# Recurrent layer: the tokens of odd chunks lie from last to first, and two chunks share each level product

## What is computed

```
def step(s, inp):                       # one chunk of one head
    qc, kc, vc, gc = inp
    cum = jnp.cumsum(gc, axis=2)        # log decay since the chunk's start, per key channel
    o_inter = einsum('bhtk,bhkv->bhtv', qc * exp(cum), s)
    decay = exp(where(causal, cum[:, :, :, None] - cum[:, :, None], -inf))
    att = einsum('bhtk,bhsk,bhtsk->bhts', qc, kc, decay)
    o = o_inter + einsum('bhts,bhsv->bhtv', att, vc)
    last = cum[:, :, -1:, :]
    s_new = exp(last)[..., None] * s + einsum('bhsk,bhsv->bhkv', kc * exp(last - cum), vc)
    return s_new, o
```

## Time and profile before

| | |
|---|---|
| median of 3 runs | 1660.47 us (1659.8 to 1665.47) |
| profiled execution | 1659.53 us, span 1657.8 us |
| PE, weight loads | 1600.0 us (97%), 1203.3 us (73%) |
| DVE | 1069.9 us (65%) |
| ACT, POOL | 651.3 us (39%), 450.1 us (27%) |
| mean granted TensorE clock | 0.988 of full speed |

### The profile page before, as it was taken

One profiled execution on the slowest core, in us unless ns is written; L12 is line 12 of the kernel. 1 busy time (PEld: TensorE's weight loads), 2 busy tenths in 40 slices (PEclk: granted clock), 3 DMA queues, 4 the chain that ended last, 5 costly groups with the idle time before them and its releaser, 6 DMA issues.

```text
span 1657.8 us, 24332 instructions
## 1 busy us (share of the span) xinstructions
PE 1600.0 (97%) x9089; PEld 1203.3 (73%) x9089; DVE 1069.9 (65%) x1962; ACT 651.3 (39%) x1252; POOL 450.1 (27%) x336
## 2 busy tenths in 40 slices
PE   6999999999999999997899999999999999998997
PEld 4788888888888887444677777777777777774543
DVE  7578787968787776213537675868777676766321
ACT  4324243424333342212145555555555455555100
POOL 5021223222122200002124343524253434323200
PEclk9999999999999999998999999999999999999999
DMA  9581819273645643423032444445453645356231
GB/s 269 151 235 60 254 42 280 61 233 104 191 131 163 207 139 117 116 74 132 13 108 77 158 151 138 137 143 166 153 166 129 194 136 185 146 193 227 89 140 40
DMA packets 254086, 242.35 MB, mean 146 GB/s; under 512 B 23162, under 2 KB 219962, under 8 KB 253970
## 3 DMA queue, kind: packets, MB, share of 16 engines
q1 hardware_dynamic: 242834, 204.21, 40.1%
q0 software_dynamic: 11136, 36.59, 6.4%
HBM read 212.63 MB, written 95.24 MB: 186 GB/s over the span
## 4 chain that ended last, share of the span: by engine, by line
PE 85%; DVE 10%; ACT 2%; issue 2%; DMA 0%; SPq 0%; POOL 0%; DVEq 0%; ACTq 0%; POOLq 0%
PE psum L1923 42%; PE psum L1947 7%; PE psum L2418 6%; PE psum L2000 6%; PE psum L2239 4%; PE psum L2216 4%; PE psum L2223 4%; PE psum L2272 2%; PE psum L1911 2%; PE psum L2178 2%; PE psum L2040 1%; PE psum L2061 1%; PE psum L2012 1%; PE psum L2054 1%; DVE arena L1265 1%
## 5 line engine op out<-in xcount | busy, mean ns | idle before, releaser
L1923 PE MATMUL psum<-arena 128*128 128x252 f32 (+1 forms) x3472 | 828.1, 389 | 5.5 <-DVE arena L1275 3.7
L1923 PEld LDWEIGHTS psum<-arena 128*128 128x128 f32 x3472 | 649.6, 193 | 131.1 <-issue 30.4
L1275 DVE TENSOR_TENSOR arena<-arena,psum 128x252 f32<-128x252 f32 (+1 forms) x310 | 130.5, 421 | 227.8 <-PE psum L1923 218.9
L816 POOL TENSOR_TENSOR arena<-arena 128x1024 f32<-128x1024 f32 x64 | 155.4, 2429 | 224.6 <-DMA arena<-k_pages 204.7
L1095 ACT ACTIVATE arena<-psum,arena 128x256 f32<-128x256 f32 (+7 forms) x128 | 93.8, 739 | 130.8 <-DVE arena L1613 130.5
L892 ACT COPY arena<-psum 128x252 f32<-128x252 f32 (+1 forms) x124 | 46.0, 371 | 235.3 <-PE psum L1923 235.3
L679 POOL TENSOR_TENSOR arena<-arena 128x512 f32<-128x512 f32 x31 | 41.0, 1323 | 292.2 <-issue 145.5
L2418 PE MATMUL psum<-arena 128*128 128x512 f32 x256 | 114.3, 597 | 0.0
L1947 PE MATMUL psum<-arena 128*128 128x512 f32 x256 | 112.7, 594 | 0.1
L2000 PEld LDWEIGHTS psum<-arena 128*128 128x128 f32 x896 | 108.1, 192 | 4.4 <-issue 1.0
L2000 PE MATMUL psum<-arena 128*128 128x64 f32 x896 | 106.1, 271 | 0.0
(11 more groups left out here) (255 smaller groups left out, 2140.8 us busy)
## 6 DMA issues: line engine op xcount, KB each, us to landing
k_pages<-in_cache_k SPq DMA_DIRECT2D x64, 512.0 KB, 6.5
v_pages<-in_cache_v SPq DMA_DIRECT2D x64, 512.0 KB, 7.1
arena<-k_pages SPq DMA_DIRECT2D x64, 512.0 KB, 3.5
arena<-v_pages SPq DMA_DIRECT2D x64, 512.0 KB, 5.4
arena<-in_w_in_a SPq DMA_DIRECT2D x32, 512.0 KB, 7.1
arena<-in_x_prompt SPq DMA_DIRECT2D x16, 512.0 KB, 6.1
arena<-in_w_kv SPq DMA_DIRECT2D x16, 512.0 KB, 5.7
arena<-in_w_in_b SPq DMA_DIRECT2D x16, 512.0 KB, 7.2
```

Of the source, the lines that this page charges most:

```text
L816: pool.tensor_tensor(k_ring[:, m % 2], k_ring[:, m % 2], q_all[:, m % S:m % S + 1, :].broadcast_to([P, PAGES, P]), ALU.mult).then_inc(kq_m ...
L1275: dve.tensor_tensor(out, more, bank[n % 2][:, 0:size(u)], ALU.add).then_inc(of.by_dve, 1)
L1923: ins = pe.matmul(bank[n % 2][:, 0:size(u)], w[:, k, :], x[:, k, :], start=(k == 0 and r in (0, 1, 3, 4)), stop=(k == HK - 1), skip_group_ ...
```

## The change

Chunks are stored in another order: the even chunks (0, 2, 4, 6) fill the first 512 columns, the odd chunks (1, 3, 5, 7) the second 512, and within an odd chunk the tokens lie from last to first. In a block of 2w columns of an odd chunk the earlier tokens (keys) now lie in the upper half, where in an even chunk they lie in the lower half. So the keys' halves of an even and an odd chunk interleave to one full array of 128 weight columns, and the queries' halves of both make 128 moving columns. `level(w)` on PE forms 4 products of 128 x 128 in place of 8 of 128 x 64; of each result, the quarter of even keys by even queries and that of odd keys by odd queries is used, chosen by the mask.

What follows from it: `x_out` writes odd tiles mirrored; the scan is two scans, the second from the last column to the first; `split` and `factors` run over even and odd chunks as an outer pair and write dense arrays; `merge` is two predicated copies of 256 columns; the masks have 128 columns a level instead of 64, the keep mask half its length; the end sums of the chunks are read from other places; the state updates and outputs take their chunk by `block_of`; `o_all` writes the odd chunks mirrored back, in three instructions instead of one; and the output projection takes tile t from `rows_of(t)`.

```diff
...
 SPLIT = (0, 252, HN)
+MID = T // 2
+def block_of(c):
+    return c % 2 * (NC // 2) + c // 2
+def mirrored(ap):
+    return bass.AP(ap.tensor, ap.offset + C - 1, [*ap.ap[:-1], [-1, C]])
+def pairs_of(ap, w, even, odd, wide=True):
+    return bass.AP(ap.tensor, ap.offset + even, [ap.ap[0], [odd - even, 2], [2 * w, MID // (2 * w)], [1 if wide else 0, w]])
 def spans(u):
...
         spare_at = used[0]
-        level_mask = area(len(LEVELS) * UPPER)
-        chunk_keep = area(T // 2).bitcast(BF16)
+        level_mask = area(len(LEVELS) * P)
+        chunk_keep = area(T // 4).bitcast(BF16)
         gain_a = area(KT)
...
         k_dec = logf[:, 0:T]
+        chunk_sums = bass.AP(cum.tensor, cum.offset + C - 1, [cum.ap[0], [MID - C + 1, 2], [C, NC // 2]])
         diffs, facts = area(2 * T), area(2 * T)
...
         prompt_out = io["state_prompt"].rearrange("l b h k v -> (l b h) k v")
+        def rows_of(t):
+            return cols(block_of(t) if t < TT else t)
         def cols(t):
...
             for l, w in enumerate(LEVELS):
-                m = level_mask[:, l * UPPER:(l + 1) * UPPER].rearrange("p (b w) -> p b w", w=w)
+                m = level_mask[:, l * P:(l + 1) * P].rearrange("p (x b w) -> p x b w", x=2, w=w)
                 last = pool.affine_select(out=m, in_=m, compare_op=ALU.is_ge, fill=0.0, base=0,
-                                          pattern=[[-2 * w, UPPER // w], [0, w]], channel_multiplier=1)
+                                          pattern=[[-w, 2], [-2 * w, UPPER // w], [0, w]], channel_multiplier=1)
             last.then_inc(built.sem, 1)
...
             pool.affine_select(out=keep, in_=keep, compare_op=ALU.not_equal, fill=0.0, base=0,
-                               pattern=[[0, NC], [1, C]], channel_multiplier=0).then_inc(built.sem, 1)
+                               pattern=[[0, NC // 2], [1, C]], channel_multiplier=0).then_inc(built.sem, 1)
             pool.wait_ge(built.sem, built.at("masks1"))
             for l, w in enumerate(LEVELS):
-                m = level_mask[:, l * UPPER:(l + 1) * UPPER].rearrange("p (b w) -> p b w", w=w)
+                m = level_mask[:, l * P:(l + 1) * P].rearrange("p (x b w) -> p x b w", x=2, w=w)
                 last = pool.affine_select(out=m, in_=m, compare_op=ALU.is_ge, fill=0.0, base=w - 1,
-                                          pattern=[[2 * w, UPPER // w], [0, w]], channel_multiplier=-1)
+                                          pattern=[[w, 2], [2 * w, UPPER // w], [0, w]], channel_multiplier=-1)
             last.then_inc(built.sem, 1)
...
                 act.activation(f_smp, logf[:, T:N], ACT.Exp)
-                act.activation(dec, cum[:, C - 1::C], ACT.Exp).then_inc(acts.sem, 1)
+                act.activation(dec.rearrange("p (x i) -> p x i", x=2), chunk_sums, ACT.Exp).then_inc(acts.sem, 1)
                 level(32)
...
                     src = bank[2 + 2 * (t % 2) + j][:, :].rearrange("p (k n) -> p k n", n=P)[:, :, 0:rows]
-                    dve.tensor_tensor(x_t[:, 4 * j:4 * j + 4, cols(t)], src,
+                    dst = x_t[:, 4 * j:4 * j + 4, rows_of(t)]
+                    dve.tensor_tensor(mirrored(dst) if t < TT and t % 2 else dst, src,
                                       gain_a[:, 4 * j:4 * j + 4].unsqueeze(2).broadcast_to([P, 4, rows]),
...
                 dve.tensor_tensor(h_new[n // 2][:, half], res[n // 2][:, half], bank[n % 2], ALU.add).then_inc(part_taken, 1)
+            def by_chunk(ap):
+                return ap.rearrange("p (i s) -> p i s", s=C)
             def o_all(h):
...
                     dve.wait_ge(o_stored, 16 * (h - 1))
-                dve.tensor_tensor(o_t[:, AH - 2 + h % 2, :], o_rs, sg_h, ALU.mult).then_inc(o_done, 1)
+                out = o_t[:, AH - 2 + h % 2, :]
+                dve.tensor_tensor(out[:, 0:MID], o_rs[:, 0:MID], sg_h[:, 0:MID], ALU.mult)
+                dve.tensor_tensor(mirrored(by_chunk(out[:, MID:T])), by_chunk(o_rs[:, MID:T]), by_chunk(sg_h[:, MID:T]), ALU.mult)
+                dve.tensor_tensor(out[:, T:N], o_rs[:, T:N], sg_h[:, T:N], ALU.mult).then_inc(o_done, 1)
             def head(h):
...
                 def split(w):
-                    c = cum.rearrange("p (b w) -> p b w", w=2 * w)
-                    d = diff[LEVELS.index(w) % 2].rearrange("p (b w) -> p b w", w=2 * w)
-                    mid = c[:, :, w - 1:w].broadcast_to([P, T // (2 * w), w])
-                    dve.tensor_tensor(d[:, :, w:2 * w], c[:, :, w:2 * w], mid, ALU.subtract)
-                    dve.tensor_tensor(d[:, :, 0:w], mid, c[:, :, 0:w], ALU.subtract).then_inc(vecs.sem, 1)
+                    d = diff[LEVELS.index(w) % 2].rearrange("p (y x b w) -> p y x b w", y=2, x=2, w=w)
+                    mid = pairs_of(cum, w, w - 1, MID + w, wide=False)
+                    dve.tensor_tensor(d[:, 1], pairs_of(cum, w, w, MID), mid, ALU.subtract)
+                    dve.tensor_tensor(d[:, 0], mid, pairs_of(cum, w, 0, MID + w), ALU.subtract).then_inc(vecs.sem, 1)
                 def factors(w):
...
                         dve.wait_ge(vecs.sem, vecs.at("q", h))
-                    d = diff[LEVELS.index(w) % 2].rearrange("p (b w) -> p b w", w=2 * w)
-                    f = fact[LEVELS.index(w) % 2].rearrange("p (b w) -> p b w", w=2 * w)
-                    q = q_h[:, 0:T].rearrange("p (b w) -> p b w", w=2 * w)
-                    k = k_h[:, 0:T].rearrange("p (b w) -> p b w", w=2 * w)
-                    dve.tensor_tensor(f[:, :, w:2 * w], d[:, :, w:2 * w], q[:, :, w:2 * w], ALU.mult)
-                    dve.tensor_tensor(f[:, :, 0:w], d[:, :, 0:w], k[:, :, 0:w], ALU.mult).then_inc(vecs.sem, 1)
+                    d = diff[LEVELS.index(w) % 2].rearrange("p (y x b w) -> p y x b w", y=2, x=2, w=w)
+                    f = fact[LEVELS.index(w) % 2]
+                    dve.tensor_tensor(f[:, MID:T].rearrange("p (x b w) -> p x b w", x=2, w=w), d[:, 1], pairs_of(q_h, w, w, MID), ALU.mult)
+                    dve.tensor_tensor(f[:, 0:MID].rearrange("p (b x w) -> p x b w", x=2, w=w), d[:, 0], pairs_of(k_h, w, 0, MID + w), ALU.mult)\
+                       .then_inc(vecs.sem, 1)
                 def merge(w):
...
                     dve.wait_ge(lv_taken_v, 9 * h + 2 + l)
-                    out = att.rearrange("p (t b w) -> p t b w", t=TT, w=2 * w)[:, :, :, w:2 * w]
-                    mask = level_mask[:, l * UPPER:(l + 1) * UPPER].bitcast(I32).rearrange("p (b w) -> p b w", w=w)
-                    dve.copy_predicated(out, mask.unsqueeze(1).broadcast_to([P, TT, UPPER // w, w]),
-                                        bank[2 + l % 2][:, :].rearrange("p (t b w) -> p t b w", t=TT, w=w))\
-                       .then_inc(lv_taken_v, 1)
+                    for x in range(2):
+                        out = att[:, MID * x:MID * x + MID].rearrange("p (i b w) -> p i b w", i=NC // 2, w=2 * w)
+                        mask = level_mask[:, l * P + x * UPPER:l * P + (x + 1) * UPPER].bitcast(I32).rearrange("p (b w) -> p b w", w=w)
+                        ins = dve.copy_predicated(out[:, :, :, 0:w] if x else out[:, :, :, w:2 * w],
+                                                  mask.unsqueeze(1).broadcast_to([P, NC // 2, UPPER // w, w]),
+                                                  bank[2 + l % 2].rearrange("p (i x b w) -> p x i b w", i=NC // 2, x=2, w=w)[:, x])
+                    ins.then_inc(lv_taken_v, 1)
                 def chunk_states(j):
...
                             ins = dve.scalar_tensor_tensor(out=s_all[:, c, :], in0=s_all[:, c - 1, :],
-                                                           scalar=dec[:, c:c + 1], in1=new, op0=ALU.mult, op1=ALU.add)
+                                                           scalar=dec[:, block_of(c):block_of(c) + 1], in1=new, op0=ALU.mult, op1=ALU.add)
                         if c % 4 == 3:
...
                 dve.wait_ge(vecs.sem, vecs.at("logf", h))
-                dve.tensor_tensor_scan(cum, chunk_keep, logf[:, 0:T], 0.0, ALU.mult, ALU.add)\
-                   .then_inc(vecs.sem, 1)
+                dve.tensor_tensor_scan(cum[:, 0:MID], chunk_keep, logf[:, 0:MID], 0.0, ALU.mult, ALU.add)
+                back = [bass.AP(ap.tensor, ap.offset + T - 1, [ap.ap[0], [-1, MID]]) for ap in (cum, logf)]
+                dve.tensor_tensor_scan(back[0], chunk_keep, back[1], 0.0, ALU.mult, ALU.add).then_inc(vecs.sem, 1)
                 a("ln_q")
...
                 fq(1)
-                c3 = cum.rearrange("p (c s) -> p c s", s=C)
-                dve.tensor_tensor(t1[:, 0:T].rearrange("p (c s) -> p c s", s=C),
-                                  c3[:, :, C - 1:C].broadcast_to([P, NC, C]), c3, ALU.subtract)\
+                halves = [ap.rearrange("p (x i s) -> p x i s", x=2, s=C) for ap in (t1[:, 0:T], cum)]
+                dve.tensor_tensor(halves[0], chunk_sums.unsqueeze(3).broadcast_to([P, 2, NC // 2, C]), halves[1], ALU.subtract)\
                    .then_inc(vecs.sem, 1)
...
                 for h in range(lo, hi):
```

(18 more changed lines are left out.)

2 lines of the change are left out of this document (1 added, 1 removed).

## The result

The changed kernel took 1603.38 us (median of 4 runs, 1602.31 to 1604.76), the kernel before 1662.97 us beside it: a ratio of 0.9639, 95% interval 0.961 to 0.9669. Run again later beside the experiments, it took 1607.77 us against 1660.46, a ratio of 0.9686 (0.9669 to 0.9703). So the change makes the kernel 3.1 to 3.6% faster, 53 to 60 us, where 44 to 47 were forecast (1616 us, range 1607 to 1628).

What follows compares the result with a forecast made beforehand. PE was taken to bound the kernel, busy 97% of the span, with DVE to watch. 47.0 - 0.7 (scan) - 2.0 (DVE late) - 0.3 (output weights) = 44.0 us saved, forecast 1616 us, range 1607 to 1628.

Steps and rivals of the forecast that it cites:

- A level costs 0.89 us: Level products on PE: 8 matmuls at 0.111 us instead of 1.73 us a level, 47.0 us saved over 56 levels.
- The rival that the product doesn't get cheaper: Level products on PE: two runs of 64 stream at half pace, level time stays, 1660 us; chance 0.03.
- Merges, mirrored writes, masks, strides: Side work on DVE and POOL: split merges +0.06 us each, 0.45 us a head; mirrored writes, masks and strides cost nothing.
- the 4.8 us by that rule alone: Ten added instructions a head, all on the path at 60 ns fixed cost each: 80 x 0.06 us lost.
- I put 2 us in all for such waits: PE waiting for DVE at level 1 or k_dec's transposes, some 1.0 us in heads without a clock fall; 2 us set aside.
- the walk: Head 1 followed through PE's and DVE's queues: level 1 doesn't wait, k_dec has 0.7 us spare, cover is thin.
- The scan at a head's start: DVE's scan split in two, on the path: 0.1 us more at each of 7 boundaries, 0.7 us lost.
- The output weights: Last head's part product needing the second half, loaded by DMA: no stall or a few tenths, 0.3 us set aside.
- The change keeps those products and shifts when they come: Clock falls behind the 8-row products, 1.7 us each: number may vary, some 6 us either way, range 1608 to 1622.

## Why the prediction was short

- **A level costs 0.89 us**: right to the hundredth, 47.0 us. Matmuls with 128 columns at the diagonal products' pace, two runs of 64 or not. The rival that the product doesn't get cheaper is out.
- **Merges, mirrored writes, masks, strides**: right. Two half merges hold DVE 0.66 us (0.67 said), halves at levels 2 and 1 share the high price, backward steps cost nothing. With all of it left in and the old products put back, the time is that of the kernel before. The fixed cost of an instruction that the Trainium skill gives in "VectorE: DVE Perf Modes", "The TRN2 errata", 60 ns, agrees with the 0.05 us that a split merge adds, though it is the table's figure for operands in SBUF: the merge reads PSUM, for which the same table has 120 cycles, an estimate of 125 ns, and the trace has less than half of that. The cost lay beside PE's work, so the 4.8 us by that rule alone didn't come. Ten instructions more a head didn't even raise DVE's busy time in the profiled execution, since other instructions met POOL's work less: the absolute values of 1032 columns take 0.70 us with POOL idle and up to 3.05 us where its sums run beside them, and had a median of 1344 ns before and 698 after. With the old levels in the new layout that median was 1344 ns again, so this follows from when the work comes and not from the layout.
- **"I put 2 us in all for such waits"**: no such wait came, and the walk had a slip. It let DVE start the addition behind the fourth F/Q product when PE had it at 177.95, and then moved PE, but not DVE, 1.7 us forward for a head without a fall. DVE was free at 177.3 by the walk's own numbers and would have had the factors at 178.8, just as PE came. The trace after has 0.2 us to spare there and 0.2 us at k_dec. But the walk was right that the cover is thin and where: 4.2 us more of DVE a head gave waits at just these places. The one wait that did appear, 1.3 us in the last head, is in a place that it had not looked at: in that head no F/Q products stand between the transposes of v and level 4 (3.4 us of PE in the others), so the 8-row products come that much sooner and wait for `v_diag`.
- **The scan at a head's start**, -0.7 us: mis-sized. The row of 3.01 us was a mean over 2.29 us (POOL idle) and 3.25 us (beside POOL), so the 2.9 ns a column of the prediction is neither. With POOL idle the halves cost 0.13 us more (1.22 + 1.20 against 2.29), close to the 0.1 said; in head 2 they held DVE 1.1 us longer, with POOL's sums beside them for 3.2 us against 1.1 us beside the whole scan. The absolute values ahead took 1.5 us less in the same head (1.35 against 2.88), and the waits of 1.0 us went. That was luck of the execution: in the later profile the absolute values took 3.0 us in head 1 and a wait of 0.5 us was there again.
- **The output weights**, -0.3 us: no product of the last head waited for them.
- **"The change keeps those products and shifts when they come"**: this failed most, and it is the step that put the measured time outside the range. The forecast took the clock falls as given and only let their number vary by chance, 6 us either way, and left them out of the 44.0 us. They depend on what PE does ahead of them, and the change rewrote that: 5 falls became 1, 6.8 us. With level 4 alone put back they return in three heads, with level 16 put back in none, with heads of the old length in none but the last, and in the old kernel they go when the two thin jobs are set apart. No single pair of runs keeps the moments of the 8-row products exactly the same, so I count over all profiled executions, by what stood ahead of and in these products with no wait of PE: the level of 1.7 us and 1.9 us of 8-row products, 12 falls in 23 heads (5 of 8, 5 of 8, 2 of 7); the level of 0.9 us and the same 1.9 us, none in 35; a dense product in between, none in 24. The thin stretch makes a fall possible and chance decides on the single one. The clock of all recorded runs agrees: the mean granted clock was 0.986 to 0.990 in the kernel before (median 0.988) and 0.989 to 0.994 in the changed one (median 0.993). In the profile before, PE had no idle time at these places. The page "TensorE: Matmul & The Clock Gate" of the Trainium skill, section "HAM oscillation — how this bites in real kernels", lays such falls to gaps in which PE waits; by it alone there should have been none here, and the measurement decides: a PE that works, thinly, has them too. The one fall after, in the last head, does stand behind a wait of 1.3 us.
- **The products behind a level**, 0.06 us each, 2.4 to 2.7 us in all: not in the sum. It shows in both directions (3.62 to 3.56 and, with 8 products put back, 3.62 again). I read it as weight loads that run ahead of their matmuls and can't while loads set the pace; no run separates this from other causes.

Together: 56.9 us came where 44.0 were summed. Of the 12.9 us between them the falls are 6.8, the products behind a level 2.4 to 2.7, the scan and the waits at the heads' starts 1.7, the DVE waits 0.7 (2.0 set aside, 1.3 came) and the output weights 0.3.

What stays open: which executions show how many falls. The kernel before ran from 1653 to 1668 us in all runs of this study, and the kernel with doubled 8-row products over 23 us, so chance has a part in the falls once the thin stretch is long enough; and the changed kernel measured 1603.4 us at one time and 1607.8 at another, with the kernel before no slower. The two profiled executions, 4.6 us apart, show where: 4.0 us arise before head 0 starts (65.71 against 61.69 us, with the granted clock at 0.50 from 25 to 32 us in the later one), 1.5 us are waits at heads' starts, and 1.7 us are saved by the last head's missing fall. Why the start differs is open.

## What to carry to other kernels

Where matmuls move fewer columns than the weights they load, count matmuls with their loads, not columns (each matmul here had its own load, so no run tells the price of the one from that of the other): pairing two half-used products saves one of them whole, and a row of the same shape elsewhere in the trace gave the new price to the hundredth. When PE's work is rewritten, look at the clock falls of the trace with the jobs that stand ahead of each: a thin stretch ahead makes falls likely, and they go or come with the edit. One profile is not enough to count them; compare the mean granted clock of all runs. In an order written out by hand, put dense work between two thin jobs.

## What was not expected of the hardware

A level of 1.7 us with 64 moving columns followed by 1.9 us of products with 8 rows brought the clock down in 12 of 23 heads, 0.9 + 1.9 us in none of 35, and twice the 8-row products (3.6 us at full clock) behind 0.9 us in all 8 of one execution, mostly for twice as long, while another execution of that kernel was 23 us faster. DVE reads and writes an operand backward at the forward pace: 1195 ns against 1224 for a scan of 512 columns with POOL idle. A predicated copy of 256 columns takes 437 ns in most levels and up to 812 at levels 2 and 1, as the whole one did (0.72 and 1.30 us).
